# Two transformer blocks in f32 on one core: 32 modulation blocks move from VectorE to TensorE, and two copies out of PSUM go ahead of a logarithm

## What is computed

```python
mod = jax.nn.silu(c) @ w_mod[l] + b_mod[l]                   # c: (1, 1024), w_mod: (1024, 6144)
mod_c = jax.nn.silu(c_ctx)[None, :] @ w_mod[l] + b_mod[l]
sh1, sc1, g1, sh2, sc2, g2 = jnp.split(mod, 6, axis=-1)
h = modulate(rms_norm(x, norm1_w[l]), sh1, sc1)              # before the input projections
...
x_mid = x + g1[:, None, :] * y                               # behind attention and mLSTM
x = x_mid + g2[:, None, :] * conv_ffn(modulate(rms_norm(x_mid, norm2_w[l]), sh2, sc2), ...)
```

## Time and profile before

| | before |
|---|---|
| median of 3 runs | 1478.62 us (1478.61 to 1483.51) |
| the profiled execution | 1478.21 us, its span 1476.4 us |
| TensorE busy | 93% of the span |
| VectorE, ScalarE, GpSimd busy | 59%, 43%, 48% |
| granted TensorE clock | 0.94 |

### The profile page before, as it was taken

How to read it: one execution, slowest core, us unless ns; L and a number is a source line. 1 busy time by engine, 2 the same in 40 slices (tenths; PEclk the granted TensorE clock), 3 DMA queues, 4 the chain that set the end, 5 groups by cost and what they waited for, 6 DMA issues and landing times. The chain is left out here.

```text
span 1476.4 us, 25250 instructions
## 1 busy us (share of the span) xinstructions
PE 1370.6 (93%) x9508; PEld 1236.3 (84%) x9508; DVE 870.7 (59%) x1409; ACT 630.6 (43%) x1043; POOL 704.6 (48%) x298
## 2 busy tenths in 40 slices
PE   5899989899997989999988999799999999799998
PEld 0688879677767979999976777799999899799998
DVE  3710154576775257776634454167777678677776
ACT  3432333232234355555543333355555444555553
POOL 1554522111116756555865500436657577556555
PEclk9899999798997989999999959899999999899999
DMA  9442421025444544455645300225556455355542
GB/s 379 147 129 86 129 72 58 29 79 171 151 146 149 162 129 168 173 172 195 211 134 151 101 14 0 86 90 198 183 175 210 129 157 157 101 174 198 183 171 101
DMA packets 57805, 208.49 MB, mean 141 GB/s; under 512 B 6640, under 2 KB 7664, under 8 KB 57472
## 3 DMA queue, kind: packets, MB, share of 16 engines
q1 hardware_dynamic: 57168, 205.55, 42.3%
q0 software_dynamic: 560, 1.88, 0.3%
HBM read 206.36 MB, written 1.05 MB: 140 GB/s over the span
## 5 line engine op out<-in xcount | busy, mean ns | idle before, releaser
L296 POOL TENSOR_TENSOR wlo<-raw,whi 128x1024 fp32r<-128x1024 f32 x284 | 697.8, 2475 | 735.8 <-ACT whi L1005 735.7
L433 PE MATMUL ps<-Hh,whi 128*128 128x256 f32 (+2 forms) x1976 | 585.6, 296 | 39.5 <-DVE Hl L1950 7.6
L434 PE MATMUL ps<-Hl,whi 128*128 128x256 f32 (+2 forms) x1976 | 575.9, 291 | 0.0
L435 PE MATMUL ps<-Hh,wlo 128*128 128x256 f32 (+2 forms) x1976 | 575.1, 291 | 0.0
L433 PEld LDWEIGHTS ps<-Hh,whi 128*128 128x128 f32 (+1 forms) x1976 | 389.0, 197 | 58.6 <-issue 26.3
L1005 ACT ACTIVATE whi<-raw 128x1024 fp32r<-128x1024 f32 x338 | 351.4, 1049 | 108.7 <-PE ps L464 39.6
L434 PEld LDWEIGHTS ps<-Hl,whi 128*128 128x128 f32 (+1 forms) x1976 | 389.7, 197 | 2.9
L435 PEld LDWEIGHTS ps<-Hh,wlo 128*128 128x128 f32 (+1 forms) x1976 | 388.8, 197 | 2.9
L1773 DVE SCALAR_TENSOR_TENSOR arena<-ps,sm,arena 128x255 f32<-128x255 f32 (+1 forms) x264 | 127.2, 483 | 100.9 <-ACT arena L1239 92.6
L433 PE MATMUL ps<-dh,whi 128*128 128x256 f32 x592 | 169.4, 286 | 11.2 <-DVE wlo L1749 4.2
L435 PE MATMUL ps<-dh,wlo 128*128 128x256 f32 x592 | 168.9, 285 | 0.0
(11 more groups left out here) (296 smaller groups left out, 1557.2 us busy)
## 6 DMA issues: line engine op xcount, KB each, us to landing
raw<-in_stream SPq DMA_DIRECT2D x386, 512.0 KB, 3.8
X<-in_xc SPq DMA_DIRECT2D x2, 1024.0 KB, 10.3
out_y<-X SPq DMA_DIRECT2D x8, 128.0 KB, 2.0
kx<-in_const POOLq DMA_DIRECT2D x1, 512.0 KB, 7.1
arena<-in_wgate POOLq DMA_DIRECT2D x1, 400.0 KB, 8.9
params<-in_params POOLq DMA_DIRECT2D x1, 372.0 KB, 7.0
k<-in_const POOLq DMA_DIRECT2D x1, 256.0 KB, 4.8
kx<-in_const POOLq DMA_DIRECT2D x1, 256.0 KB, 4.3
```

Source lines behind the costliest of these rows:

```text
L296: pool.tensor_tensor(wlo[:, slot, :], raw[:, rslot, :], whi[:, slot, :].bitcast(f32), ALU.subtract).then_inc(rest_done[0], 1)
L433: pe.matmul(out, lh, rh, start=start, stop=False, skip_group_check=True)
L434: pe.matmul(out, lh, rl, start=False, stop=False, skip_group_check=True)
L435: return pe.matmul(out, ll, rh, start=False, stop=stop, skip_group_check=True)
```

## The change

The 32 later modulation blocks are no longer multiplied on VectorE in the attention, but on TensorE in the stage of the input projections, in 8 batches of 4, behind the jobs 1, 2, 3, 5, 7, 9, 11 and 13 (MOD_BATCHES: where TensorE does them, behind which weight block they stand in the stream, how many). Their layout in HBM is now that of the first 16: 128 inputs by 1024 outputs, 8 blocks per section. Each block is four products with the same c_cols, each over 256 columns, into four groups of 32 partitions of bank 3. Sections use the two halves of that bank in turn. ScalarE copies each finished section into the unused half of X (SECT_AT, behind `evac(q)` with its splits for q = 2, 5, 9 and 13), and the first block of the next section waits for that copy (sect_out). Behind job 15 eight transposes turn the sections (mod_turns), and VectorE adds the biases to MODB there. Four small transposes move from bank 3 to bank 2.

The row c_kept, its loads, Silu, products and copies are gone, and so is c_lat. In the stream no modulation block stands behind a gm job, and the weight blocks 5 to 17 have up to 32 modulation blocks between them. `splittable` counts the batches that are already done. And ScalarE does evac(0) and evac(1), with their splits, ahead of the gate's Abs, Exp and Ln.

```diff
+MOD_BATCHES = [(q, q + 3, 4) for q in (1, 2, 3, 5, 7, 9, 11, 13)]
+SECT_AT = (2, 5, 9, 13)
+STREAM = [("mod", n) for n in range(MOD_FIRST)]
+_n = MOD_FIRST
+for _s in range(S_BRANCH):
+    STREAM.append(("w", _s))
+    for _, _behind, _count in MOD_BATCHES:
+        if _behind == _s:
+            STREAM += [("mod", _n + _i) for _i in range(_count)]
+            _n += _count
...
-            for half in range(2):
-                pool.dma_start(c_kept[half], crow_d[:, 512 * half:512 * half + 512]).then_inc(s_crow, 16)
...
-        def splittable(q, made=MOD_FIRST):
+        def splittable(q):
+            made = MOD_FIRST + sum(count for at, _, count in MOD_BATCHES if at <= q)
...
+            def mod_batch(count):
+                for n in range(mods[0], mods[0] + count):
+                    sect, k = divmod(n - MOD_FIRST, KC)
+                    if k == 0 and sect > 0:
+                        pe.wait_ge(S["sect_out"], sect)
+                    r = RAW_OF_MOD[n]
+                    wait_raw(pe, r)
+                    for j in range(4):
+                        mm = pe.matmul(PS[32 * j:32 * j + 32, 3, T * (sect % 2):T * (sect % 2) + T], c_cols[:, k, :],
+                                       raw[:, r % RING, T * j:T * j + T], start=k == 0, stop=k == KC - 1)
+                    mm.then_inc(mod_used, 1)
+                mods[0] += count
+            def mod_turns():
+                pe.wait_ge(S["sect_out"], 4)
+                pe.wait_ge(S["ut_ready"], 1)
+                for sect in range(4):
+                    for half in range(2):
+                        at = P * (2 * (sect % 2) + half)
+                        mm = pe.transpose(PS[:, 2 + sect // 2, at:at + P], X[:, sect, T + P * half:T + P * half + P],
+                                          ident)
+                mm.then_inc(S["sect_t"], 1)
...
-            for q in range(2, 28):
-                gp_job(q)
+            for q in range(1, 28):
+                if q >= 2:
+                    gp_job(q)
+                for at, _, count in MOD_BATCHES:
+                    if at == q:
+                        mod_batch(count)
+                if q == 15:
+                    mod_turns()
...
             pe.wait_ge(S["comb_done"], 28)
-            pe.wait_ge(S["c_kept"], 2)
-            for half in range(2):
-                pe.matmul(PS[:, 6 + half, :], ones[64:65, :], c_kept[half], start=True, stop=True)\
-                  .then_inc(S["c_bc"], 1)
...
-            act.wait_ge(s_crow, 32)
-            for half in range(2):
-                act.activation(c_kept[half], c_kept[half], ACT.Silu).then_inc(S["c_kept"], 1)
...
+            evac(0)
+            evac(1)
+            fl = slice(64, GATE_P)
+            act.activation(gl[fl], gt[fl], ACT.Abs).then_inc(S["gate_act"], 1)
...
             for q in range(28):
-                evac(q)
+                if q >= 2:
+                    evac(q)
+                if q in SECT_AT:
+                    sect = SECT_AT.index(q)
+                    act.wait_ge(mod_used, MOD_FIRST + KC * (sect + 1))
+                    act.activation(X[:, sect, T:2 * T], PS[:, 3, T * (sect % 2):T * (sect % 2) + T], ACT.Copy)\
+                       .then_inc(S["sect_out"], 1)
...
             for q in range(MO):
+                if q == 16:
+                    dve.wait_ge(S["sect_t"], 1)
+                    for b in range(2):
+                        modb_add(b)
                 evac(q)
...
-            for half in range(2):
-                dve.wait_ge(S["c_bc"], half + 1)
-                dve.tensor_copy(c_lat[:, 512 * half:512 * half + 512], PS[:, 6 + half, :]).then_inc(S["c_moved"], 1)
...
-                    r = RAW_OF_MOD[MOD_FIRST + u]
-                    wait_raw(dve, r)
-                    dve.scalar_tensor_tensor(raw[:, r % RING, :], raw[:, r % RING, :], 1.0, c_lat, ALU.mult, ALU.mult,
-                                             accum_out=MODB[:, u:u + 1]).then_inc(mod_done, 1)
...
-            dve.wait_ge(mod_done, 4 * KC)
-            link(dve.tensor_tensor(MODB[:, :], MODB[:, :], pr("b_mod", 16, 48), ALU.add))
```

More of the change, by code:

```diff
@@ L36 @@
 GM0 = W_IN_JOBS.index("gm")
-STREAM = [("mod", n) for n in range(MOD_FIRST)] + [("w", s) for s in range(GM0)]
-for _j in range(KC):
-    STREAM += [("w", GM0 + _j)] + [("mod", MOD_FIRST + 4 * _j + n) for n in range(4)]
+MOD_BATCHES = [(q, q + 3, 4) for q in (1, 2, 3, 5, 7, 9, 11, 13)]
[8 more added lines that the diff above has]
+            _n += _count
 STREAM += [("w", s) for s in range(S_BRANCH, S_END)]
@@ L197, in build @@
         mixT = [work[:, 1024 + 256 * s:1280 + 256 * s] for s in range(2)]
-        s_par, s_crow, s_ccol, s_x, s_k0, s_kx, s_kx2, s_wg, s_wf = (sem(n) for n in (
-            "params_in", "crow_in", "ccol_in", "x_in", "const_in", "const1_in", "const2_in", "wgate_in", "wf_in"))
+        s_par, s_ccol, s_x, s_k0, s_kx, s_kx2, s_wg, s_wf = (sem(n) for n in (
+            "params_in", "ccol_in", "x_in", "const_in", "const1_in", "const2_in", "wgate_in", "wf_in"))
         s_x = [s_x, sem("x_in2")]
@@ L227, in build @@
             "sb_arg", "sb_wm", "sb_out", "fox_max", "fox_pt", "fox_out", "t2_lo", "mix_cu", "fin", "wg_lo",
-            "spread_ready", "v_chain", "c_kept", "c_moved",
-            "c_bc", "mod_t", "mod_copy", "ss_ready", "gates_ps", "u_t", "st_done", "bc_done", "qk_done", "pv_done", "rot_done", "sc_done",
+            "spread_ready", "v_chain", "sect_out", "modb_done",
+            "sect_t", "mod_t", "mod_copy", "ss_ready", "gates_ps", "u_t", "st_done", "bc_done", "qk_done", "pv_done", "rot_done", "sc_done",
             "tr_done", "av_done", "t_ps", "gates2_ps", "fin_bc", "z_done", "r_done", "sbv_done", "fs_done",
@@ L1111, in evac @@
                     act.activation(sqr[i % 2][:, 0:n], PS[:, bank, 0:n], ACT.Square).then_inc(S["qk_sq"], 1)
-                splits_upto(splittable(q, made))
-            for q in range(28):
-                evac(q)
+                splits_upto(splittable(q))
+            evac(0)
+            evac(1)
+            fl = slice(64, GATE_P)
+            act.activation(gl[fl], gt[fl], ACT.Abs).then_inc(S["gate_act"], 1)
+            act.wait_ge(S["gate_act"], 1)
+            act.activation(gl[fl], gl[fl], ACT.Exp, scale=-1.0).then_inc(S["gate_act"], 1)
+            act.wait_ge(S["gate_act"], 2)
+            act.activation(gl[fl], gl[fl], ACT.Ln, bias=1.0).then_inc(S["gate_act"], 1)
+            for q in range(28):
+                if q >= 2:
[5 more added lines that the diff above has]
+                       .then_inc(S["sect_out"], 1)
                 if q == 6:
@@ L1459, in norm, with modb_add @@
                                                      ALU.add, ALU.subtract).then_inc(S["hl_done"], 1)
+            def modb_add(b):
+                turned = PS[:, 2 + b, :].rearrange("p (s h j r) -> p s j h r", s=2, h=2, j=4)
+                dve.tensor_tensor(MODB[:, 16 * b:16 * b + 16].rearrange("p (s j h) -> p s j h", s=2, j=4),
+                                  turned[:, :, :, :, 0], pr("b_mod", 16 + 16 * b, 32 + 16 * b)
+                                  .rearrange("p (s j h) -> p s j h", s=2, j=4), ALU.add).then_inc(S["modb_done"], 1)
             first_norm()
@@ L2008, in layout @@
     first = w_mod[:, 0:2 * D].reshape(KC, P, 2, D).transpose(0, 2, 1, 3).reshape(2 * KC, P, D)
-    mod = np.concatenate([first, w_mod.T.reshape(6 * KC, P, D)[2 * KC:]])
+    mod = np.concatenate([first, w_mod[:, 2 * D:].reshape(KC, P, 4, D).transpose(2, 0, 1, 3).reshape(4 * KC, P, D)])
     rows = np.concatenate([np.arange(HD * h, HD * h + HD) for h in order])
```

39 lines of the change are left out of this document (12 added, 27 removed).

## The result

| | before | after |
|---|---|---|
| median | 1478.76 us (1478.03 to 1483.51, 6 runs) | 1491.58 us (1486.17 to 1496.91, 6 runs) |
| the profiled execution | 1478.21 us, span 1476.4 | 1496.91 us, span 1495.0 |
| granted clock | 0.94 | 0.945 |

The account below looks back on a forecast made before the run. TensorE, busy 93% of the span, was taken as the bound. Projections lose 22.2 us and attention gains 13.4, so +8.8 on the profiled 1478.21 us, 0.4 below the runs' median: forecast 1487.5 us, range 1474 to 1499.

Parts of the forecast that it names:

- products and transposes: Input projections, TensorE: 32 blocks at 0.48 us, going in and out of 8 batches, and 8 transposes add 17.9 us.
- waits behind jobs 3, 5, 7: Input projections: TensorE waits 3.5, 0.9 and 2.3 us for row copies standing behind splits that wait for loads, 6.7 together.
- half clock behind them: Input projections: half clock follows the 3.5 us wait, and the 2.3 us wait in half of the cases, +2.6 us.
- idle ahead of job 2 and its half clock: Input projections: copies first and the first batch remove 3.3 us of TensorE idle and 1.7 us of half clock.
- projections: The whole input projections stage: 17.9 + 6.7 + 2.6 - 3.3 - 1.7 = 22.2 us lost.
- attention: Attention with its gate jobs: removing 32 multiply-adds from VectorE gains 13.4 us, bounds 8 and 24.
- the walk of the landings: Projections' loads: 3.6 us from issue to landing, 1.28 between queued landings; block 7 lands at 75.3, row copy ends 78.1.
- Six periods: Attention: each four-unit period takes 13.95 + 0.95 + 0.6 = 15.5 us against 16.7; six save 7.3 us.
- the last stretch: End of attention: 24.05 us becomes 18.1, saving 5.9 us.
- The split of the 1.5 us into 0.95 and 0.45: Attention, a unit that loses time: about 0.95 us belong to GpSimd's pass holding the minimum, 0.45 to the multiply-add.
- Rival C: Attention runs at TensorE's own pace, giving back 24 us instead of 13.4: 1477 us; chance 0.12.
- Rival B: Projections: row copies don't hold TensorE, so waits and half clock behind them go, 9.3 us less: 1478 us; chance 0.17.

Follow-up runs that it names:

- e13: The changed kernel once more, no edit: 1500.77 us, median of four runs; ratio to before 1.0124, from the three without the longest.
- e1: The changed kernel with ScalarE's copy of a finished modulation section moved ahead of evac(q) and its splits: 1484.4 us, ratio to before 1.0032.
- e2: The kernel before with only the reordering, evac(0) and evac(1) ahead of the gate's Abs, Exp and Ln: 1477.87 us, ratio 0.9977.
- e10: e1 with a block's four products in one column group for 7 of 8 blocks per section (results wrong): 1521.75 us, ratio to before 1.0295.
- e7: e1 without VectorE's minimum with the sink in attention: 1474.1 us, ratio to before 0.9952.
- e5: The kernel before without VectorE's minimum with the sink, multiply-adds kept: 1480.86 us, ratio 0.9995.
- e12: The kernel before with VectorE's multiply-add over 8 of 1024 columns, all loads kept: one run of 1469.87 us, beside 1478.36 of its comparison.
- e9: e7 with the last section's 8 modulation blocks moved behind job 27: 1472.9 us, ratio to before 0.9941.
- e11: e9 with its splits there moved behind the first exponentials and at most two per job: 1474.92 us, ratio to before 0.9976.

## Why the prediction was right, point by point

The sign and the mechanism held, and by the medians so did the size: 12.8 us more than before, where 8.8 were forecast, and slower was the likeliest of the three. The profiles are less kind. In them the two stages add up to 28.0 - 10.4 = +17.6 us, and +16.8 in e13, twice the 22.2 - 13.4 = +8.8 of the sum, and both stages miss on the same side. Both are profiles of the longest run of their kernel, so how much of this a run at the median has stays open; that the median came out 4 us from the forecast is in part luck. The terms:

| term | forecast | measured |
|---|---|---|
| products and transposes | +17.9 | +18.2 (e1 against e2) |
| waits behind jobs 3, 5, 7 | +6.7 | +11.1, again +10.0 |
| half clock behind them | +2.6 | up to +5.4, again +1.3 |
| idle ahead of job 2 and its half clock | -5.0 | -5.0; by reordering alone -3.1 |
| projections | +22.2 | +28.0, again +24.0 |
| attention | -13.4 | -10.4, again -7.2 |

TensorE also came to the first batch 0.7 us earlier than before (58.9, not 59.6), which nothing in the change explains: it was 59.5 in e1 and 59.7 in e13. With it the measured terms add up to 29.0, 1.0 over the stage's 28.0, as the half clock is an upper bound.

*The products.* Four blocks take 1.93 us, and the next job starts 1.87 behind the batch's start; with 0.11 that the job ahead of it takes longer (5.66 us for job 2 in e1, 5.55 in e2) that is 2.0 us per batch, forecast as 2.1. No idle time is left at 59.6 to 62.9: job 2 starts at 60.72, and the clock is 1.00 until 78.2.

*The waits.* The mechanism was the forecast one, sect_out behind the splits behind the loads, and so were its two places. Its price was 1.7 times too low. The mis-sized step is the walk of the landings. It took 3.6 us from issue to landing for the first load of a batch and 1.28 between landings. The distances between landings hold. But the first load of the second batch, issued at 67.08, landed at 73.68: 6.6 us. The one before it had landed at 69.08. In e13 the same load took 6.57 us, in e1 3.83, but there the next one, released 0.43 us later, took 6.41. So block 7, walked to 75.3, landed at 77.4, and with it the copy. The rows of loads for 60 to 180 us of after, and for 67 to 76.5:

```profile
raw<-in_stream SPq DMA_DIRECT2D x51, 512.0 KB, 6.2
...
raw<-in_stream SPq DMA_DIRECT2D x5, 512.0 KB, 7.4
```

The median of a stage with 26 loads, 3.6 us, was no price for one with 51 at a DMA share of 0.58. Why nothing landed between 69.1 and 73.7 isn't settled; between 68 and 73 the DMA engines were busy at 0.82 to 0.95 and moved 168 to 389 GB/s.

*The half clock.* I priced it by the one stretch of 3.41 us behind a wait of 3.3. Behind 6.1 and 4.5 us it was 6.83 us each, of which TensorE worked 4.98 and 5.79; behind e13's 6.1 it was 3.41. So its length doesn't follow from the wait's. The forecast of 2.6 lies between the two measured values, 5.4 and 1.3, and that is chance.

*The attention.* Six periods came out at 15.52 us each (359.13 to 452.23), forecast 15.5; the minimum is held once in each, 1.84 us. A period with no fall of the clock takes 14.84 us, summed as 13.95 + 0.95 = 14.9. The other 0.68 is the clock, forecast 0.6, and here luck helped: the same attention had no fall in e10, two in after and three in e13. But the first four units took 13.6 instead of the 12.4 that I had left unchanged: they now have a pass over a minimum too, the one shown above at 354.48. And the last stretch took 19.6 instead of 18.1, with 4.9 us at half clock in it. The falls of the clock are fewer, two in the stage where before has six, but each is 6.83 us long. The split of the 1.5 us into 0.95 and 0.45 did no harm here, since the multiply-add alone went and took 0.55 us per period with it; for the minimum alone it would have been wrong, 0.20 instead of 0.95. Rival C's price, 24 us for an attention in which GpSimd's pass holds nothing, was right: e7 has 24.2. Its condition, that the minimum no longer meets the pass, isn't given in after, as I had argued.

*Rival B* (no waits for the row copy) is e1: 1484.4 us beside 1481.1 of its comparison, where I gave 1478, that is 0.6 under 1478.62. In its profile 3.0 us of waits are left in the projections, and its attention (126.20 us) gives 10.4 instead of 13.4. These 6.0 us are more than the 3.9 by which the medians miss B.

## What to carry to other kernels

Count a moved piece of work twice: its own time on the new engine, and what its loads and its result's copy do to the order of the others; here the second was 11 us of waits in 28, and one copy moved ahead of the stalled splits gave 8 of them back, and no half clock followed. Where one engine's pass holds another, don't split the lost time among the operations that are late. Whichever comes first takes most of it, and taking out one lets the next one in: 11 and 4.5 us alone were 24 together, and 0.55 and 0.20 us of a period 1.52. And idle time in the middle of a chain is only worth as much as the loads and splits around it allow.

## What the runs showed of the hardware

- While GpSimd subtracts 128 x 1024 (2.35 us), a VectorE operation with two inputs in SBUF hardly moves: in each case seen it ended behind the pass by no more than its own time. 128 x 1 took 1.84 us instead of 0.16 and ended with the pass, 128 x 128 2.11 instead of 0.29, 128 x 256 2.42 instead of 0.42, and the multiply-add of 1024 columns 2.87 instead of 1.21, 1.08 behind the pass. Maximum and copy, which read PSUM alone, kept a mean of 0.68 to 0.69 us in attention in e5, e7, e12 and after, and 0.69 and 0.68 inside a pass in e7.
- Four column groups of 32 with all 128 rows run side by side: 0.48 us for a block against 1.77 in one group.
- Where and how long the clock falls is not the same in two executions of the same kernel: after had 13.7 us of half clock in attention and 126 us for the stage, e13 20.5 and 129. e10, whose attention has the same program and the same waits, had none and 120. e7, e9 and e11, without the waits behind the held minimum, had none, and 112.47, 112.48 and 112.46 us.
